# Five feed-forward layers with two block pairs in seven products each, sums made by accumulating loads, and buffers given in pairs at the joints

## The reference

```python
def swiglu(x, w_gate, w_up, w_down):
    return (jax.nn.silu(x @ w_gate) * (x @ w_up)) @ w_down
```

## Time and profile before

| What | Value |
| --- | --- |
| median of 3 runs | 1622.52 us (1622.01 to 1623.05) |
| profiled execution | 1622.12 us |
| its span, first to last instruction | 1620.3 us |
| TensorE busy | 1598.5 us, 99% |
| VectorE busy | 1096.2 us, 68% |
| ScalarE busy | 819.2 us, 51% |
| POOL busy | 87.8 us, 5% |
| moved by DMA | 306.79 MB, mean 189 GB/s |
| mean granted clock of TensorE | 0.997 of full |

### The profile page before, as it was taken

The page is one execution under the profiler, slowest core; times in us unless marked ns, Lnnn a source line. Parts: engine busy times, 40 slices in busy tenths (PEclk is TensorE's granted clock), DMA queues, the critical chain, the costliest instruction groups (busy, mean ns, idle before and its releaser), DMA issues.

```text
span 1620.3 us, 18778 instructions
## 1 busy us (share of the span) xinstructions
PE 1598.5 (99%) x7719; PEld 1330.9 (82%) x7719; DVE 1096.2 (68%) x1055; ACT 819.2 (51%) x857; POOL 87.8 (5%) x104
## 2 busy tenths in 40 slices
PE   9999999999999999999999999899999999999998
PEld 7888897788888788888988888788888998888886
DVE  6974656679853789637668865578546666698653
ACT  6644547655642766434654654255433435446550
POOL 0241000000000000001010000000000132000000
PEclk9999999999999999999999999999999999999999
DMA  9774674466652866544657656557355654675650
GB/s 326 210 217 148 200 234 145 163 215 208 202 193 100 282 198 198 166 151 147 235 183 229 195 178 216 164 164 226 130 208 186 204 182 145 206 246 160 197 190 26
DMA packets 222100, 306.79 MB, mean 189 GB/s; under 512 B 8896, under 2 KB 144320, under 8 KB 221888
## 3 DMA queue, kind: packets, MB, share of 16 engines
q1 hardware_dynamic: 217232, 290.29, 54.9%
q0 software_dynamic: 4416, 15.05, 3.0%
q10 hardware_dynamic: 368, 0.27, 0.1%
HBM read 304.52 MB, written 1.05 MB: 189 GB/s over the span
## 4 chain that ended last, share of the span: by engine, by line
PE 82%; DVE 11%; issue 3%; ACT 2%; DMA 1%; SPq 0%; DVEq 0%; ACTq 0%
PE bank L785 23%; PE bank L798 23%; PE bank L789 20%; DVE split L1817 6%; PE bank L735 3%; PE bank L802 3%; DVE whole L1821 2%; PE bank L881 2%; PE bank L883 2%; PE bank L884 2%; ACT split L1385 1%; PE bank L847 1%; PE bank L849 1%; PE bank L852 1%; ACT sh L1564 0%
## 5 line engine op out<-in xcount | busy, mean ns | idle before, releaser
L1817 DVE TENSOR_TENSOR split<-whole,split 128x2048 fp32r<-128x2048 f32 (+2 forms) x314 | 670.6, 2158 | 266.9 <-ACT split L1385 265.3
L1385 ACT ACTIVATE split<-whole 128x2048 fp32r<-128x2048 f32 (+1 forms) x298 | 550.8, 1871 | 219.9 <-PE bank L798 80.2
L785 PE MATMUL bank<-split,xh 128*128 128x512 f32 x1212 | 329.7, 394 | 0.0
L798 PE MATMUL bank<-split,xh 128*128 128x512 f32 x1212 | 324.8, 390 | 0.0
L789 PE MATMUL bank<-split,xl 128*128 128x512 f32 x1040 | 278.4, 389 | 0.0
L798 PEld LDWEIGHTS bank<-split,xh 128*128 128x128 f32 x1212 | 227.2, 188 | 47.9 <-DVE split L1817 0.2
L785 PEld LDWEIGHTS bank<-split,xh 128*128 128x128 f32 x1212 | 223.7, 188 | 47.5 <-issue 3.0
L789 PEld LDWEIGHTS bank<-split,xl 128*128 128x128 f32 x1040 | 195.2, 188 | 41.4
L785 PE MATMUL bank<-split,th 128*128 128x512 f32 x524 | 145.4, 396 | 0.0
L789 PE MATMUL bank<-split,tl 128*128 128x512 f32 x524 | 142.7, 391 | 0.0
L798 PE MATMUL bank<-split,th 128*128 128x512 f32 x524 | 142.2, 389 | 0.0
(11 more groups left out here) (306 smaller groups left out, 1527.8 us busy)
## 6 DMA issues: line engine op xcount, KB each, us to landing
whole<-in_ffn_w_in SPq DMA_DIRECT2D x176, 512.0 KB, 5.1
whole<-in_ffn_w_out SPq DMA_DIRECT2D x40, 1024.0 KB, 5.1
whole<-in_ret_w_in SPq DMA_DIRECT2D x24, 1024.0 KB, 5.1
whole<-in_ffn_w_gate SPq DMA_DIRECT2D x42, 512.0 KB, 4.3
whole<-in_ffn_w_up SPq DMA_DIRECT2D x42, 512.0 KB, 6.0
whole<-in_ffn_w_down SPq DMA_DIRECT2D x20, 1024.0 KB, 5.1
whole<-in_w_in SPq DMA_DIRECT2D x16, 1024.0 KB, 5.5
whole<-in_gla_w_in SPq DMA_DIRECT2D x12, 1024.0 KB, 5.8
```

The costliest lines, as they stand in the source:

```text
L785: pe.matmul(o[:, :], tokens(0, k), whi[:, k, :], start=start and k == 0, stop=False, skip_group_check=True)
L798: ins = pe.matmul(o[:, :], tokens(0, k), wlo[:, k, :], start=False, stop=end, skip_group_check=True)
L1385: act.activation(split[s][:, 0:n], whole[r][:, 0:n], ACT.Copy).then_inc(hi.mark(i), 1)
L1817: dve.tensor_tensor(split[r][:, c0:c1], whole[r][:, c0:c1], split[s][:, c0:c1].bitcast(F32), ALU.subtract).then_inc(lo.mark(*what), 1)
```

## The change

The steps exist in two orders. ONE_PAIR is for f1 and differs from before by the place of turns 4, 6, 3 and 7. TWO_PAIRS is for f2, a0, a1, b0, b1: pairs (3, 4) and (7, 8) in seven products each, and only 0, 1, 2, 5, 6, 9 and 10 as tiles. Class Order holds a list, its pairs, and the positions of the tiles.

Signs are changed so that the weight sums are additions: t1 = B12 + B11 and t3 = B12 + B22 are made by loading one addend (SP) and adding the other by a load with accumulation from POOL's queue (pool_sum), two pieces of 512 KB each; t2 = B22 + t1 and t4 = B21 + t2 stay with VectorE. So t1 has a load of its own. load_key sets t1's load ahead of b11's. In f1 the two accumulating loads stand in the list of bias gathers, at n = 2 and n = 6; elsewhere behind the gains of the joint.

The tokens for the sums (xs) are copied from the banks of the transposes by ScalarE (act_tokens) in f2 to b1, and TensorE waits for that copy before it uses such a bank again.

ScalarE splits up to ahead(i, 1), with buffers set free by tile i - 1 or earlier. VectorE follows up to behind(i), one tile less, and within a product step makes them after the addition of the result, before the multiply.

Layer f2 has block 13 as well. The first four tiles of f2 to b1 and the last eight of every layer take slots (fixed pairs of buffers).

```diff
@@ -34,18 +32,42 @@
     ("product", 0, "t1"), ("tile", 5, 1), ("turn", 2),
     ("product", 0, "t2"), ("tile", 6, 0),
     ("product", 0, "b22"), ("tile", 6, 1), ("turn", 5), ("p",),
-    ("product", 0, "t3"), ("tile", 7, 0), ("turn", 4),
-    ("product", 0, "b21"), ("tile", 7, 1), ("turn", 6),
-    ("product", 0, "t4"), ("tile", 8, 0), ("tile", 8, 1), ("turn", 3), ("turn", 7),
+    ("product", 0, "t3"), ("tile", 7, 0),
+    ("product", 0, "b21"), ("tile", 7, 1), ("turn", 6), ("turn", 4),
+    ("product", 0, "t4"), ("tile", 8, 0), ("tile", 8, 1), ("turn", 7), ("turn", 3),
     ("tile", 9, 0), ("tile", 9, 1), ("turn", 8),
     ("tile", 10, 0), ("tile", 10, 1), ("turn", 9))
+TWO_PAIRS = (
+    ("tile", 0, 0), ("tile", 0, 1), ("tile", 1, 0), ("tile", 1, 1), ("turn", 0),
+    ("token sums",),
+    ("tile", 2, 0), ("product", 0, "b11"), ("blocks",), ("tile", 2, 1), ("turn", 1), ("tile", 5, 0),
+    ("product", 0, "t1"), ("product", 0, "t2"), ("tile", 5, 1), ("turn", 2), ("p",),
+    ("product", 0, "b22"), ("product", 0, "t3"), ("tile", 6, 0),
+    ("product", 0, "b21"), ("product", 0, "t4"), ("turn", 4), ("tile", 6, 1), ("turn", 5),
+    ("product", 1, "b11"), ("turn", 3), ("tile", 9, 0),
+    ("product", 1, "t1"), ("product", 1, "t2"), ("tile", 9, 1), ("turn", 6),
+    ("product", 1, "b22"), ("product", 1, "t3"), ("tile", 10, 0), ("turn", 9),
+    ("product", 1, "b21"), ("product", 1, "t4"), ("turn", 8), ("tile", 10, 1), ("turn", 7))
 LEAD_STEPS = 5
-PLAIN = [what[0] for step, *what in FFN_STEPS if step == "tile" and what[1] == 0]
-TURNED = [what[0] for step, *what in FFN_STEPS if step == "turn"] + [PLAIN[-1]]
-
-
-def last_turned(j):
-    return max([n for n in (j - 1, j) if n >= 0], key=TURNED.index)
+
+
+class Order:
+
+
+    def __init__(self, steps, *pairs):
+        self.steps, self.pairs = steps, pairs
+        self.plain = [what[0] for step, *what in steps if step == "tile" and what[1] == 0]
+        self.turned = [what[0] for step, *what in steps if step == "turn"] + [self.plain[-1]]
+
+    def place(self, j):
+        return self.plain.index(j)
+
+    def last_turned(self, j):
+        return max([n for n in (j - 1, j) if n >= 0], key=self.turned.index)
+
+
...
                     g, m = what
-                    j = FFN_PAIRS[g]
+                    j = ORDER[name].pairs[g]
                     spot[name, g, m] = i = len(tiles)
                     product_of[i] = (name, g, m)
                     plan(name + "gu", {"b11": gate_up(j, 0), "b21": gate_up(j, 1), "b22": gate_up(j + 1, 1),
-                                       "t3": gate_up(j + 1, 0)}.get(m, []), 4)
+                                       "t1": gate_up(j + 1, 0), "t3": gate_up(j + 1, 0)}.get(m, []), 4)
+                    if m in ("t1", "t3"):
+                        addend[i] = gate_up(j, 0) if m == "t1" else gate_up(j + 1, 1)
                     if m == "t4":
                         grp = group[name, g] = Group(j, j + 1, *(spot[name, g, m] for m in Group._fields[2:]))
-                        load_key[grp.t3], load_key[grp.b22], load_key[grp.b21] = (
-                            grp.b11 + 0.5, grp.t1 - 0.1, grp.t2 - 0.1)
+                        load_key[grp.t1], load_key[grp.t3], load_key[grp.b22], load_key[grp.b21] = (
+                            grp.b11 - 0.9, grp.t2 + 0.5, grp.t1 - 0.1, grp.t2 - 0.1)
             plan_rows(name + "d", wd_, 22)
 
         def plan_ffn_2(name, i, j):
...
-        def give_ffn(first, end, among, into_mixer=False):
-
-            closing = 6 if into_mixer else 0
-            give_blocks(first, end - closing, among)
-            if closing:
-                slots = [s for s in (5, 6) if SLOT[s][0] in among]
-                give_slots(end - 6, end, [[slots[i - 2]] if 0 <= i - 2 < len(slots) else range(5) for i in range(6)])
-
-        give_ffn(0, at["mvx"][0], range(12), True)
+        def give_ffn(name, among, into_mixer=False):
+
+            first, end = at[name + "gu"][0], at[name + "d"][-1] + 1
+            slots = [s for s in range(7) if SLOT[s][0] in among and SLOT[s][1] in among]
+            lead = first + (0 if name == "f1" else 4)
+            give_slots(first, lead, [slots] * 4)
+            give_blocks(lead, end - 8, among)
+            if into_mixer:
+                closing = [[s] for s in slots if s >= 5]
+                give_slots(end - 8, end, [slots] * 2 + [range(5)] * 2 + closing + [range(5)] * (4 - len(closing)))
+            else:
+                give_slots(end - 8, end, [slots] * 8)
+
+        give_ffn("f1", range(12), True)
         give_slots(at["mvx"][0], at["f2gu"][0], range(5))
         block_age[10] = block_age[11] = (at["mo"][0] - 0.5, (vec, ("merged", 1, 1)))
-        give_ffn(at["f2gu"][0], at["pp"][0], range(12))
+        block_age[13] = (at["mo"][0] - 0.4, (vec, ("merged", 1, 1)))
+        give_ffn("f2", (*range(12), 13))
         give_slots(at["pp"][0], at["a0gu"][0], range(6))
-        block_age[12] = block_age[13] = (at["pp"][1], None)
-        give_ffn(at["a0gu"][0], at["gv"][0], range(14), True)
+        block_age[12] = (at["pp"][1], None)
...
@@ -491,12 +523,16 @@
             elif of >= 0:
                 eng.wait_ge(passed.sem, passed.of(of, 1))
 
-        def ahead(i):
+        def ahead(i, gap=2):
 
             j = i
-            while j + 1 < NT and j < i + 5 and needed[j + 1] <= i - 2:
+            while j + 1 < NT and j < i + 5 and needed[j + 1] <= i - gap:
                 j += 1
             return j
+
+        def behind(i):
+
+            return max(i, ahead(i, 1) - 1)
 
         halved = {0, 1}.union(*(e.late for e in edges))
 
@@ -612,6 +648,20 @@
             pool.dma_start(gain[:, g % GAINS, :], gain_src[g].broadcast_to([P, D])).then_inc(
                 gain_in[g % GAINS].mark(g), 16)
 
+        def pool_sums(pool, name):
+            for n in range(len(ORDER[name].pairs)):
+                for m, i in (("t1", group[name, n].t1), ("t3", group[name, n].t3)):
+                    pool_sum(pool, m, i)
+
+        def pool_sum(pool, m, i):
+            b = load_to[i]
+            dst = lanes(whole[b][:, :], 4)
+            pool.wait_ge(raw_in[b].sem, raw_in[b].of(i))
+            if sum_in[m].n:
+                pool.wait_ge(sum_in[m].sem, sum_in[m].n)
+            for src, c0 in addend[i]:
+                pool.dma_start(dst[:, :, c0:c0 + 256], src, accum_op=ALU.add).then_inc(sum_in[m].mark(i), 16)
+
         def pool_program(pool):
             pool.memset(ident[:, :], 0.0).then_inc(gp.mark("zeros"), 1)
             pool.wait_ge(gp.sem, gp.of("zeros"))
@@ -635,6 +685,10 @@
 
             pool.dma_start(mask[:, :], A["c_mask"]).then_inc(bias_in[0].mark("mask"), 16)
             for n in range(8):
+                if n == 2:
+                    pool_sum(pool, "t1", group["f1", 0].t1)
+                if n == 6:
+                    pool_sum(pool, "t3", group["f1", 0].t3)
                 pool.wait_ge(lo.sem, lo.of(6 + n))
                 pool_bias(0, n)
             for n in range(8):
@@ -660,10 +714,12 @@
...
@@ -725,6 +784,8 @@
             if len(uses) >= 2:
                 old, emptied = uses[-2]
                 pe.wait_ge(emptied.sem, emptied.of(*old))
+                if old[0] == "x" and old[1] in ORDER and old[1] != "f1":
+                    pe.wait_ge(fn.sem, fn.of("xs", *old[1:]))
             bank_of[key] = bank[4 + len(uses) % 2]
             uses.append((key, by))
             return bank_of[key]
...
@@ -1371,7 +1433,9 @@
                 i = fed["hi"]
                 fed["hi"] += 1
                 n, r, s = tiles[i].k * tiles[i].width, load_to[i], high_to[i]
-                if i in product_of and product_of[i][2] in SUMS:
+                if i in addend:
+                    act.wait_ge(sum_in[product_of[i][2]].sem, sum_in[product_of[i][2]].of(i))
+                elif i in product_of and product_of[i][2] in ("t2", "t4"):
                     act.wait_ge(vec.sem, vec.of("sum", i))
                 else:
                     act.wait_ge(raw_in[r].sem, raw_in[r].of(i))
@@ -1392,6 +1456,12 @@
         def act_turn_x(act, nx, t):
             for g in range(2):
                 act_turned(act, ("x", nx, t, g), xh[:, 4 * g:4 * g + 4, t * P:(t + 1) * P])
+
+        def act_tokens(act, nx, t):
+            for g in range(2):
+                act.wait_ge(turn_lo.sem, turn_lo.of("x", nx, t, g))
+                act.activation(xs[t][g], lanes(bank_of.get(("x", nx, t, g), bank[4])[:, :], 4), ACT.Copy).then_inc(
+                    fn.mark("xs", nx, t, g), 1)
 
         def act_turn_in(act, t, g, K=range(4)):
 
...
@@ -1485,19 +1557,22 @@
                 act_turn_x(act, stage, 1)
             unit(1, 0)
             act_high(act, ahead(four[1]))
+            if stage in ORDER:
+                act_tokens(act, stage, 1)
             unit(0, 1)
             act_high(act, ahead(four[3]))
             unit(1, 1)
             act_high(act, ahead(four[3] + 1))
 
         def act_ffn(act, f, e):
```

(29 more changed lines are left out.)

112 lines of the change are left out of this document (63 added, 49 removed).

## The result

The changed kernel takes 1610.12 us (median of 4 runs, 1606.73 to 1610.72), the kernel before 1622.51 us on the same chip. The ratio is 0.9919, 95% interval 0.9902 to 0.9936: 0.8% faster. The medians lie 12.4 us apart; the ratio, which rests on all runs (one of the four, 1606.73, lies low), gives 13.1 us. The forecast was 1607, with 1595 to 1615 as its range.

A forecast was written before the change was run, and what follows sets the result against it. TensorE, busy 99% of the span, was taken as the bound. Terms -13.6 - 6.0 - 5.4 - 4.2 + 3.4 + 10.2 = -15.6 us took the profiled 1622.1 to 1606.5, median 1606.9; likeliest 1607, range 1595 to 1615.

The forecast's parts named there:

- The second pair: Gate and up in f2 to b1: one unit of 12 matmuls less on TensorE per layer, 13.6 us saved.
- Joints: a1 to b0 and f2 to projection: buffer pairs end TensorE's waits, saving 6.0 and 5.4 us; idle alone 7.8.
- The turn of block 4: Five layers, f1 included: moved behind a later product, this turn no longer waits for VectorE's multiply, saving 4.2 us.
- VectorE keeps up: First pair, f2 to b1: low parts ready before TensorE wants them; cost zero, bound 1 us a layer.
- Accumulating loads cost nothing in f2 to b1: Sums of t1 and t3 land before ScalarE needs them, so the cost is zero.
- Token copies: Lead of f2 and a0: TensorE's transposes wait for ScalarE's copies, costing 2.4 and 1.0 us, sum 3.4.
- The first layer: f1: t1's accumulating load goes out late behind POOL's second bias gather, delaying TensorE's third group; cost 10.2 us.
- Rival (a): f1 isn't late: POOL's load goes out in time or VectorE reaches load 7's low near 46; 1596.7 us, chance 0.16.
- Rival (b): VectorE misses t2 or tile (5, 1) by about 1 us in each of five layers: 1612, chance 0.16.
- Rival (c): Accumulating load moves at half a plain one's rate; f1 pays 3.2 us more, other layers nothing: 1610, chance 0.12.
- Rival (d): Accumulating load far slower; time above 19 us paid in each of ten pairs, some 50 us slower at 24; chance 0.08.
- Rival (e): Joints don't close because the next tiles' first loads are late; TensorE keeps 11.4 us: 1618, chance 0.03.

The follow-up runs named there:

- the kernel with one pair: Changed kernel with all six layers on the one-pair order, accumulating loads, joint slots and ScalarE token copies kept: 1621.84 us, ratio 0.9992.
- the kernel with the joints alone: Kernel before, with buffer pairs for the last eight down tiles of f2 and a1 and b0's first four tiles: 1611.24 us, ratio 0.9925.
- joints undone: Changed kernel with single blocks by age again for the last eight down tiles in layers no mixer follows: 1632.21 us, ratio 1.0052.
- plain loads: Changed kernel with the accumulating loads of t1 and t3 made without the addition, same bytes, blocks and queue: 1606.14 us, ratio 0.9895.
- sum twice: Changed kernel with VectorE forming t4's sum twice in the first pair of f2 to b1: 1614.94 us, ratio 0.9952.
- t1's load ahead: Changed kernel with t1's accumulating load issued ahead of the first bias gather in f1: 1599.43 us, ratio 0.9853.
- the same with the limits: t1's load ahead, plus the kernel before's limits on ScalarE's and VectorE's splitting ahead in f1: 1597.39 us, ratio 0.9843.
- added twice: Changed kernel with each accumulating load of t1 and t3 in f2 to b1 issued twice, one behind the other's landing: 1732.21 us, ratio 1.0671.

## Why the prediction was right, point by point

**The second pair, -13.6 us.** Right; 13.0 by the kernel with one pair.

**Joints, -6.0 and -5.4 us.** Right: 6.0 and 5.6 by the kernel with the joints alone. The upper reading, with the slow clock, was the right one against the bound of 7.8 us for the idle alone.

**The turn of block 4, -4.2 us.** Its waits are gone. In a1, b0 and b1 the stretches came out 0.1 to 0.2 us better than pair, turn and joint together. Two small errors cancel in that: by the kernel with one pair the pair gives 2.6 us a layer and not 2.72, and the turn, with whatever else changed there, 1.0 to 1.2 us (b0: 173.16 before, 172.01) and not 0.85.

**VectorE keeps up, 0.** Right, and the working was good to a few tenths: t2's low part in f2 had 0.5 us to spare (forecast 0.2) and in a0 2.1 (forecast 24.0 - 21.9 = 2.1). Doubling one sum turned it into waits. Rival (b) is refuted.

**Accumulating loads cost nothing in f2 to b1.** Right, with less room than I thought: of 19 us the addition used 8.5 to 14.8.

**Token copies, +3.4 us.** Place and waits were right (2.2 and 0.8 us of idle). The size was low in f2: TensorE ran its transposes and the first group behind them at the slow clock, and the stretch lost about 4 us in place of 2.4. This is the 1.3 us by which f2 missed. That a stall is followed by a slow clock I had priced at the joints, and forgot here.

**The first layer, +10.2 us.** This is the term that was mis-sized: it measured 13.0 (12.16 and the 0.8 of the turn). The chain is as I told it, and the experiment that moved one call took 11 us of it away. Of the 2.8 us, 1.2 is the issue (53.06 against 51.9; 0.36 of it is a later start, from the tokens' own load at the very start) and 1.1 the landing (7.9 against 6.8). With these t1's third group comes 2.2 us late. The other 0.5 us are lost behind it, where TensorE still runs at the slow clock. The 6.8 us, from the nearest plain row, lay between the 5.4 us of a plain load at this place and the 7.9 of one with the addition, so part of the addition's price was in it by luck. Rival (a) is refuted for this kernel: neither of its conditions was met, since POOL's load went out at 52.3 and VectorE had load 7's low part only at 51.3. Its time of 1596.7 is near what the kernel takes (1597.4) once the load goes out early and the limits of before are back; with the load alone it takes 1599.4.

**Rival (c).** Its time, 1610, is the one measured. Its mechanism is there too: the addition costs 2.2 times the engines' time and 3.3 us in f1. But the landing grew by 2.5 to 2.7 us and not by 3.2 from 6.8, and the rest of the distance to the forecast is the clock in f2, the wait in the mixer and the start. So that its time is met so closely is in part luck. I had the right bound and gave it too little weight. **Rival (d)** asks for more than 19 us; a doubled addition goes past it, and each pair then pays, as it said. **Rival (e)** is refuted.

**What I did not have.** The 0.9 us in the mixer behind a0: a low part on VectorE stands ahead of its copy of the gate's columns, and the tile for it landed 3.7 us behind its neighbour in place of 2.7. With one pair a layer it vanishes; how the second pair delays that landing wasn't tried.

## What to carry to other kernels

A load issued by an engine that also waits for others is as late as the slowest wait ahead of it in that engine's program: before moving work onto such a queue, walk through everything that stands in front, since one call moved by two places was worth 11 us here, nearly as much as 60 matmuls. When a buffer is freed late, look at both ends of it, the split that fills it and the load that must land first. Price a stall of TensorE with what follows it at the slow clock, and price a transfer whole, from its first issue to its last landing under the traffic of its place, not by the median of its parts.

## What the hardware showed that I had not expected

- The same accumulating load of 1 MB took 7.9 us from its second issue at 53 us, and 15.2 us from 36.6 us, beside SP's loads. Nearly alone on the engines (53 to 61 us of the changed kernel) it kept them 93% busy and moved 148 GB/s; the plain load at its place (52.4 to 57.9) moved 217 GB/s at 72%.
- The accumulating loads went out in packets of 1 KB, the plain ones of the same shape in packets of 4 KB.
- The same stall of 2.2 us in f2 was followed by a group of eight transposes that took 1.57 to 1.94 us, at the lower clock, in five kernels (the changed one, one pair, joints undone, plain loads, sum twice), and 1.11 to 1.12 us in three others (t1's load ahead, the same with the limits, added twice). What decides it the traces don't show; it is worth about 1.5 us (f2's stretch 202.39 us in the changed kernel, 200.84 in the one with t1's load ahead). The windows of the changed kernel and of that one, just behind the stall (busy us of PE, PEld, DVE, ACT, POOL; granted clock; DMA share; GB/s):

```profile
373.00:376.00 3.00, 3.00 (x11) 2.58 (x10) 1.38 (x2) 2.51 (x4) 0.13 (x1) 0.54 1.08 349
```

```profile
362.00:365.00 3.00, 3.00 (x17) 2.51 (x15) 1.50 (x3) 2.73 (x4) 0.15 (x1) 1.00 1.08 352
```

The granted clock is 0.54 in the one, so 1.2 GHz for most of the window, and 1.00, 2.4 GHz, in the other, behind the same work and the same stall.
